# Gate columns in a recurrence tile that is worked first, and 512-column products for the recurrence's output

## What is computed

```python
proj = h @ w_in
(rx, rgate, q, kc, vc, ks, vs, kw, vw, nsa_g, mg_rnn, mg_attn) = jnp.split(proj, splits, axis=-1)
hr = rg_lru(causal_dwconv(rx, rnn_conv_w, rnn_conv_b), rg_w_a, rg_b_a, rg_w_x, rg_b_x, lru_lambda)
y_rnn = (hr * jax.nn.gelu(rgate)) @ w_rnn_out
o = nsa(q, kc, vc, ks, vs, kw, vw, nsa_g, ...)      # g = sigmoid(gates); g0*o_cmp + g1*o_slc + g2*o_win
y_attn = o @ w_attn_out
x = x + (jax.nn.sigmoid(mg_rnn) * y_rnn + jax.nn.sigmoid(mg_attn) * y_attn) @ w_out
```

## Time and profile before

| | us |
|---|---|
| median of 3 runs | 818.85 (818.69 to 819.10) |
| the profiled execution | 818.65 |
| its span, first to last instruction | 816.9 |

### The profile page before, as it was taken

One profiled execution on the slowest core, in us unless ns is written; L12 is line 12 of the kernel. 1 busy time (PEld: TensorE's weight loads), 2 busy tenths in 40 slices (PEclk: granted clock), 3 DMA queues, 4 the chain that ended last, 5 costly groups with the idle time before them and its releaser, 6 DMA issues.

```text
span 816.9 us, 12246 instructions
## 1 busy us (share of the span) xinstructions
PE 806.0 (99%) x4997; PEld 705.7 (86%) x4997; DVE 588.0 (72%) x751; ACT 481.8 (59%) x730; POOL 31.3 (4%) x46
## 2 busy tenths in 40 slices
PE   9999999999999999999999999999999999999996
PEld 8889898889899998988888888888888988888885
DVE  5684597898966775798787868877877655654555
ACT  6463687878757444675666556446654644544551
POOL 1103000000000000000000000020110000000000
PEclk9999999999999999999999999999999999999998
DMA  8436442332434674446555554674443555555431
GB/s 329 155 125 261 164 170 101 120 115 106 154 119 159 228 275 164 142 168 213 200 172 189 206 203 162 234 258 148 155 178 133 207 206 186 179 214 195 162 148 51
DMA packets 22631, 144.00 MB, mean 176 GB/s; under 512 B 2608, under 2 KB 3120, under 8 KB 8240
## 3 DMA queue, kind: packets, MB, share of 16 engines
q1 hardware_dynamic: 20880, 137.92, 47.6%
q10 hardware_dynamic: 1696, 5.31, 1.8%
HBM read 142.17 MB, written 1.05 MB: 175 GB/s over the span
## 4 chain that ended last, share of the span: by engine, by line
PE 92%; ACT 3%; DVE 3%; issue 1%; POOL 0%; DVEq 0%; POOLq 0%; ACTq 0%
PE PS L1689 19%; PE PS L1693 10%; PE PS L1742 10%; PE PS L1743 10%; PE PS L1746 10%; PE PS L1676 7%; PE PS L1677 6%; PE PS L1681 6%; PE PS L1705 2%; PE PS L1836 1%; PE PS L2006 1%; PE PS L1802 1%; PE PS L1813 1%; PE PS L1713 1%; DVE WL L1040 1%
## 5 line engine op out<-in xcount | busy, mean ns | idle before, releaser
L1040 DVE TENSOR_TENSOR WL<-RAW,WH 128x2048 fp32r<-128x2048 f32 (+2 forms) x128 | 285.2, 2229 | 45.5 <-ACT WH L614 45.5
L614 ACT ACTIVATE WH<-RAW 128x2048 fp32r<-128x2048 f32 (+2 forms) x128 | 238.8, 1867 | 67.5 <-PE PS L1746 26.5
L1445 DVE TENSOR_TENSOR HLS<-PS,HLS 128x512 f32<-128x512 f32 x46 | 31.7, 689 | 92.7 <-ACT HLS L945 92.7
L1689 PE MATMUL PS<-CHL,WH 128*128 128x512 f32 x352 | 87.9, 392 | 0.0
L1676 PE MATMUL PS<-BHL,WH 128*126 128x256 f32 (+2 forms) x344 | 85.6, 287 | 0.4 <-ACT TI L785 0.4
L1677 PE MATMUL PS<-BHL,WH 128*126 128x256 f32 (+2 forms) x344 | 83.6, 282 | 0.0
L945 ACT ACTIVATE HLS<-PS 128x512 f32<-128x512 f32 x46 | 27.4, 595 | 90.8 <-PE PS L1693 86.3
L1689 PE MATMUL PS<-BHL,WH 128*128 128x512 f32 x320 | 79.9, 392 | 0.0
L1689 PEld LDWEIGHTS PS<-CHL,WH 128*128 128x128 f32 x352 | 63.9, 189 | 11.8
L1676 PEld LDWEIGHTS PS<-BHL,WH 128*126 128x126 f32 (+2 forms) x344 | 64.3, 187 | 5.2 <-issue 4.3
L1743 PE MATMUL PS<-WH,AL 128*128 128x512 f32 x176 | 68.7, 391 | 0.0
(11 more groups left out here) (312 smaller groups left out, 1374.9 us busy)
## 6 DMA issues: line engine op xcount, KB each, us to landing
RAW<-in_w_stream SPq DMA_DIRECT2D x108, 1024.0 KB, 4.8
RAW<-in_w_stream SPq DMA_DIRECT2D x11, 1008.0 KB, 4.8
RAW<-in_w_stream SPq DMA_DIRECT2D x8, 704.0 KB, 4.3
WF<-in_w_stream SPq DMA_DIRECT2D x2, 1024.0 KB, 5.0
LN<-in_ln ACTq DMA_DIRECT2D x2, 1024.0 KB, 5.3
WF<-in_w_stream SPq DMA_DIRECT2D x4, 294.0 KB, 2.8
X<-in_x SPq DMA_DIRECT2D x2, 512.0 KB, 4.2
RAW<-in_w_stream SPq DMA_DIRECT2D x2, 512.0 KB, 7.2
```

The costliest lines, as they stand in the source:

```text
L614: eng.activation(WH[:, c % NSLOT, 0:CHUNKS[c][2]], raw(c), ACT.Copy).then_inc(w_hi, 1)
L1040: eng.tensor_tensor(WL[:, c % NSLOT, 0:CHUNKS[c][2]], raw(c), f32(WH[:, c % NSLOT, 0:CHUNKS[c][2]]), ALU.subtract).then_inc(w_lo, 1)
L1445: eng.tensor_tensor(HLS[:, n % 4, :, :], PS[:, bank:bank + 2, 0:TOK], HLS[:, n % 4, :, :], ALU.add)\
L1689: eng.matmul(PS[:, bank, :], wh, HL[:, k, :, :].rearrange("p a t -> p (a t)"), start=(k == 0), stop=False)
```

## The change

The gate chunk goes. Its 48 columns are put, 24 each, in rows 96 to 119 of the two halves (rx and rgate) of rnn tile 4, which is moved to the front of the recurrence, behind w1 1. W0 is now that tile, and the order is rnn 4, rnn 0, rnn 1, mg 0, ri 0, rnn 2, rnn 3, mg 1, ri 1; from there on it is as before. ACT applies the Tanhs at the end of window 0, once DVE's conv steps of that tile are done; PE transposes them in window 1, DVE makes `gts` in window 2. GTT is zeroed on DVE. The rows' waits count tiles in the new order (`RNN_NO`, `RNN_THROUGH`). For group 0, A, squares and roots fall in window 5, and the exponentials of the compressed scores in window 4. Key transposes of cmp 1 use banks 2 and 3 as those of cmp 0 do. AH and AL lie side by side in AHL; a ro chunk is 11 products of 512 columns and 11 of 256, and DVE adds both halves in three steps.

The diff, cut to its core (left out: the new waits on `RNN_NO` and `RNN_THROUGH`, sizes, the packing of the weights):

```diff
@@ -39,6 +39,9 @@
 RG_OF = [(g, t) for g, n in enumerate(RG_TILES) for t in range(n)]
+GATE_TILE = RG_AT[RG_TILES.index(3)] + 2
+GATE_ROW = 96
+GATE_COLS = 24
@@ -89,14 +92,14 @@
     out += [("cmp", i, CHUNK, True) for i in range(2)]
-    out += [("gate", 0, KD * 3 * NH, True)]
...
     out += [("w1", i, CHUNK, False) for i in range(2)]
+    out += [("rnn", GATE_TILE, 2 * KD * RP, True)]
...
         out += [("mg", mg + n, CHUNK, True) for n in range(ahead)]
-        out += [("rnn", RG_AT[g] + t, 2 * KD * RP, True) for t in range(RG_TILES[g])]
+        out += [("rnn", i, 2 * KD * RP, True) for i in range(RG_AT[g], RG_AT[g + 1]) if i != GATE_TILE]
@@ -127,7 +130,10 @@
 OFFS = [sum(P * w for _, _, w, _ in CHUNKS[:c]) for c in range(NCH + 1)]
-W0 = AT[("rnn", 0)]
+W0 = AT[("rnn", GATE_TILE)]
+RNN_NO = {i: n for n, i in enumerate(i for kind, i, _, _ in CHUNKS if kind == "rnn")}
+RNN_THROUGH = [max(RNN_NO[i] for i in range(RG_AT[g + 1])) + 1 if g >= RG_TILES.index(3) else
+               max(RNN_NO[i] for i in range(RG_AT[g], RG_AT[g + 1])) + 1 for g in range(NG)]
@@ -198,8 +204,10 @@
+    if step >= 2 and W0 + w - step + 1 == AT["ri", 0]:
+        return 0
     kind, g, _, _ = CHUNKS[max(0, W0 + w - step)]
-    return g if kind == "ri" else None
+    return g if kind == "ri" and (g or step < 2) else None
@@ -259,8 +267,8 @@
         a_at = top[0]
-        AH = put("AH", [P, NA, TOK], F32R)
-        AL = put("AL", [P, NA, TOK], F32R)
+        AHL = put("AHL", [P, NA, 2, TOK], F32R)
+        AH, AL = AHL[:, :, 0, :], AHL[:, :, 1, :]
@@ -664,6 +673,12 @@
                                    accum_out=css[0:NKV * CP, :]).then_inc(kc_sq, 1)
+                    eng.wait_ge(hk_zero, 6)
+                    eng.wait_ge(mb_dve, 1)
+                    for part in range(2):
+                        eng.activation(GTT[32 * part:32 * part + GATE_COLS, :],
+                                       PS[GATE_ROW:GATE_ROW + GATE_COLS, mb_of(MB_NO[W0]), TOK * part:TOK * part + TOK],
+                                       ACT.Tanh, scale=0.5).then_inc(gate_tanh, 1)
@@ -676,6 +691,9 @@
                     eng.activation(SCT[:, :], PS[:, 5, :], ACT.Copy).then_inc(kcz_ready, 1)
+                if w == 4:
+                    eng.wait_ge(sc_sub, 1)
+                    eng.activation(SC[:, :, :, :], SC[:, :, :, :], ACT.Exp).then_inc(sc_exp, 1)
@@ -742,9 +760,6 @@
                         eng.activation(l2[0:RP, :], l1[0:RP, :], ACT.Exp, scale=-1.0).then_inc(lam_exp, 1)
-                if kind == "gate":
-                    eng.wait_ge(chunk_done, c + 1)
-                    eng.activation(GTT[:, :], PS[0:3 * NH, 4, 0:TOK], ACT.Tanh, scale=0.5).then_inc(gate_tanh, 1)
@@ -761,8 +776,10 @@
                         eng.activation(HK[:, 0, :, 0:NC], hidden(0), ACT.Gelu_apprx_tanh).then_inc(hk_ready, 1)
-                if kind == "rnn" and i == 1:
+                if c == W0 + 1:
                     q_copy(1)
+                if c == W0:
+                    eng.wait_ge(q_ss, 2 * NT)
@@ -1007,16 +1024,13 @@
                     split(c + 2)
-                if c == SPLIT_IN_SOFTMAX:
+                if c == SPLIT_AHEAD:
                     split(c + 2)
-                if c - W0 == 4:
-                    eng.wait_ge(sc_sub, 1)
-                    eng.activation(SC[:, :, :, :], SC[:, :, :, :], ACT.Exp).then_inc(sc_exp, 1)
...
                 side(c)
-                if CHUNKS[c][0] == "ri" and c != SPLIT_IN_SOFTMAX:
+                if CHUNKS[c][0] == "ri" and c != SPLIT_AHEAD:
@@ -1150,8 +1164,12 @@
                         last.then_inc(vb_ready, 1)
+                if w == 2:
+                    eng.wait_ge(gate_t_done, 1)
+                    eng.tensor_scalar(gts[:, :].rearrange("p (t a n) -> p t a n", t=NT, a=2),
+                                      PS[:, 4, TOK:2 * TOK - P].rearrange("p (t a n) -> p t a n", t=NT, a=2)[:, :, :, 0:GATE_COLS],
+                                      0.5, 0.5, ALU.mult, ALU.add).then_inc(gate_ready, 1)
                 if w == 3:
-                    split(W0 + w + 2)
@@ -1208,11 +1226,12 @@
                     eng.tensor_tensor(JJ[:, :], ident[:, 0:64], ident[:, 64:P], ALU.add).then_inc(hk_zero, 1)
+                    eng.memset(GTT[:, :], 0.0).then_inc(hk_zero, 1)
...
                     eng.wait_ge(gk_ready, 1)
-                    bank = (2, 6)[i]
+                    bank = 2
@@ -1229,8 +1248,8 @@
                     eng.scalar_tensor_tensor(q, p, -8.0, q, ALU.mult, ALU.add).then_inc(c4_ready, 1)
-                if kind == "gate" or kind == "q" and i == 0:
-                    n = 0 if kind == "gate" else 1
+                if kind == "q" and i < 2:
+                    n = i
@@ -1273,8 +1288,12 @@
                     t = MG[:, i, :]
-                    link(eng.scalar_tensor_tensor(t, t, 1.0, PS[:, bank, 0:256], ALU.add, ALU.mult))
-                    eng.tensor_tensor(t, t, MG[:, 8 + i, :], ALU.add).then_inc(m_ready, 1)
+                    if i >= 1:
+                        eng.wait_ge(m_ready, i)
+                    link(eng.scalar_tensor_tensor(RS2[:, :, :], t.unsqueeze(1).broadcast_to([P, 2, TOK]), 1.0,
+                                                  PS[:, bank, :].rearrange("p (a t) -> p a t", a=2), ALU.add, ALU.mult))
+                    link(eng.tensor_tensor(t, RS2[:, 0, :], MG[:, 8 + i, :], ALU.add))
+                    eng.tensor_tensor(t, t, RS2[:, 1, :], ALU.add).then_inc(m_ready, 1)
@@ -1605,9 +1624,7 @@
                     unit_max(u)
-                if c - W0 == UNIT_WINDOWS[0]:
-                    compressed_weights()
-                if c and CHUNKS[c - 1][0] == "ri" and c - 1 != SPLIT_IN_SOFTMAX:
+                if c and CHUNKS[c - 1][0] == "ri" and c - 1 != SPLIT_AHEAD:
@@ -1615,6 +1632,8 @@
                     rg_log_a(G)
+                if c - W0 == UNIT_WINDOWS[0]:
+                    compressed_weights()
@@ -1631,7 +1650,7 @@
                     rg_second(NG - 1)
-                if CHUNKS[c][:2] not in SUMS_FIRST and kind != "ri":
+                if CHUNKS[c][:2] not in SUMS_FIRST and kind != "ri" or c == SPLIT_AHEAD:
@@ -1858,6 +1877,11 @@
                                   ident[0:NKV * CP, 0:NKV * CP]).then_inc(kct_done, 1)
+                    eng.wait_ge(gate_tanh, 2)
+                    for t in range(NT):
+                        last = eng.transpose(PS[:, 4, TOK + 64 * t:TOK + 64 * t + 64], GTT[:, P * t:P * t + P],
+                                             ident[0:64, 0:64])
+                    last.then_inc(gate_t_done, 1)
@@ -1968,15 +1992,11 @@
                         last = f_tile(PS[:, bank, 256 * j:256 * j + 256], c, 1024 * j, P, BH, BL)
-                if kind == "gate":
-                    eng.wait_ge(const_in, 32)
-                    eng.wait_ge(kn_ready, 2)
-                    eng.wait_ge(k_sq, 2)
-                    last = f_tile(PS[0:3 * NH, 4, 0:TOK], c, 0, 3 * NH, BH, BL)
...
                     if i == 0:
-                        eng.wait_ge(kt_copied, 2)
+                        eng.wait_ge(kn_ready, 2 * NT)
+                        eng.wait_ge(k_sq, 2 * NT)
@@ -1989,6 +2009,8 @@
                 if kind == "rnn":
+                    if c == W0 + 2:
+                        eng.wait_ge(gate_tanh, 2)
@@ -2041,7 +2063,14 @@
                     bank = mb_bank(MB_NO[c])
-                    last = f_tile(PS[:, bank, 0:256], c, 0, P, AH, AL, nk=NR, parts=RP)
+                    s = c % NSLOT
+                    for k in range(NR):
+                        eng.matmul(PS[:, bank, :], WH[0:RP, s, P * k:P * k + P], AHL[0:RP, k, :, :].rearrange("p a t -> p (a t)"),
+                                   start=(k == 0), stop=False)
+                    eng.wait_ge(w_lo, SPLIT_NO[c] + 1)
+                    for k in range(NR):
+                        last = eng.matmul(PS[:, bank, 0:TOK], WL[0:RP, s, P * k:P * k + P], AH[0:RP, k, :], start=False,
+                                          stop=(k == NR - 1))
@@ -2182,8 +2211,6 @@
-                if n == 0:
-                    eng.wait_ge(gate_ready, 1)
@@ -2195,22 +2222,19 @@
                 if kind == "cmp":
+                    eng.wait_ge(const_in, 32)
                     eng.wait_ge(kn_ready, 2 * i + 2)
+                    if i:
+                        eng.wait_ge(kt_copied, 1)
...
                             o = 256 * (g % 2) + P * t
-                            last = eng.transpose(PS[:, (2, 6)[i] + g // 2, o:o + P],
+                            last = eng.transpose(PS[:, 2 + g // 2, o:o + P],
...
                     last.then_inc(kt_done, 1)
-                if kind == "q" and i == 0:
-                    eng.wait_ge(gate_tanh, 1)
-                    for t in range(NT):
-                        last = eng.transpose(PS[:, 4, TOK + 3 * NH * t:TOK + 3 * NH * t + 3 * NH], GTT[:, P * t:P * t + P],
-                                             ident[0:3 * NH, 0:3 * NH])
-                    last.then_inc(gate_t_done, 1)
...
                     q_transposes(0)
```

(28 more changed lines are left out.)

## The result

The kernel after takes 820.46 us (median of 17 runs, 819.2 to 821.31), the kernel before in the same session 818.85 (17 runs, 818.69 to 819.96). The ratio is 1.0016, 95% interval 1.001 to 1.0023: slower by 1.6 us. The interval leaves out 1, so the loss is real, but it is small: 0.16%. The forecast was 817.3 with a range up to 818.9. The kernel after also scatters over 2.1 us, while 15 of the 17 runs of before lie within 0.41 us; the reason for that turns out to be part of the loss. The profiled execution of after took 819.2 us (span 817.5), which is the fastest of its 17, so its trace shows less of the loss than the other runs have.

A forecast was written before the change was run, and what follows sets the result against it. PE was taken as the bound, busy 806.0 of 816.9 us. Terms -3.31 + 0.3 + 2.85 - 0.43 - 0.96 = -1.55 took the profiled 818.65 to 817.10; 0.20 for the median gave 817.3 us, range 815.2 to 818.9.

The forecast's parts named there:

- Part 3: Window 1, the main step: PE waits for ACT's q copy, queued behind the Tanhs and mg 0's split; +2.85 us.
- Part 1: Ahead of W0: gate chunk and its transposes go, so PE reaches W0 3.31 us earlier; q 0's load hidden.
- Part 2: Window 1: the gates' two transposes return on PE, +0.3 us (0 to 0.5).
- Part 4: Ahead of rnn 2: PE's stall for the bank ACT reads goes, -0.43 us (-0.43 to 0).
- Part 5: Recurrence output: a ro chunk goes from 3.96 to 3.84 us, saving 0.96 us for 8; DVE's added work fits.
- Part 6: Windows 3 to 7: reordered work adds nothing, 1.5 us slack ahead of mg 1; unit 3's 0.4 us stall stays.
- B: Rival, window 1: the wait is short or absent; 814.5 us, or 815.9 with half of it; chance 0.14.
- C: Rival, ro chunks: DVE becomes their bound, slower; 822.6 us at 4.5 us a chunk; chance 0.08.
- D: Rival, ro chunks: the output change does nothing, chunks stay at 3.96 us; 818.3 us; chance 0.08.

The follow-up runs named there:

- experiment 8: Kernel after with PE's start-up products changed from 14 of 128 columns to 13 of 128 and 16 of 8, 60 more PE instructions: 818.46 us, ratio 0.9997.
- experiment 3: Kernel after with thirty unused transposes of a constant on PE ahead of its wait in window 1: 818.33 us, ratio 0.9995.
- experiment 5: Kernel before with only the change's ro output part (11 products of 512 columns, 11 of 256, three DVE steps): 817.69 us, ratio 0.9988.
- experiment 1: Kernel after with ACT's copy of the transposed q moved into window 0, ahead of the gates' Tanhs and the split of mg 0: 814.70 us, ratio 0.9951.
- experiment 9: Kernel after with both the copy of q ahead of the Tanhs and 60 more PE instructions at the start: 814.02 us, ratio 0.9943.
- experiment 6: Kernel after with the recurrence's output part undone, 33 products of 256 columns in a ro chunk again: 821.81 us, ratio 1.0038.

## Why the prediction was wrong

The mechanism forecast as the main step is what happened: the change wins at the gate chunk, at rnn 2 and in ro, and pays it back in window 1, behind the copy of q. Two terms were wrong, one in size and one by its absence.

**Part 3, the size.** 2.85 us forecast, 3.84 measured in after, 4.4 and 4.6 in two relatives. The step that failed is that part 3 goes "by the times of before; all of it shifts by the same 3.31", which carries the landing at 82.00 over unchanged; the rivals defend it with "the same load, queue and trigger as before". The load's trigger moved with the work, but the code load that it shares the DMA engines with did not, and the load landed 0.85 us later than the shift said. With the code load out of the way (experiment 8) the wait is 2.97, 0.12 over the forecast.

**The clock, missing.** The prediction reads the granted clock once, finds 1.00, and from then on prices a wait at its own length. It adds a wait of 2.85 us to a kernel whose longest standing of PE in this part was 0.43 us, and doesn't ask what the clock does behind it. So the step that failed is a term put at nothing: the clock behind the wait. It costs some 1.4 us in the profiled execution of after and 2.1 at the median (experiment 3). No row of before could give that price, since the clock never falls there in this stretch; but the range should have had an end for it, and has none. Even with the right wait it would have been needed: experiment 8 has 2.97 us, and seven of its 11 runs show the fall by their times and mean clocks.

The two together: 817.3 + 1.0 + 2.1 = 820.4, measured 820.46. The 2.1 is itself the difference of two medians, 820.46 and 818.33, so what this sum tests is the rest: 817.3 + 1.0 = 818.3 against the 818.33 of experiment 3. And where neither acts, in the four runs of experiment 8 at a mean clock of 0.997, the time is 817.1, against 818.71 for the kernel before beside it: 1.6 us less, where the sum says 1.55.

**Part 1**: W0 3.26 us earlier, forecast 3.31. Right, q 0 starts at 45.52 and its load is hidden. **Part 2**: with the clock at 1.00 the transposes and what stands with them take 89.30 to 90.19, 0.89, in experiment 3, against 0.69 before (88.40 to 89.09): 0.20, forecast 0.3. **Part 4**: no idle time ahead of rnn 2 (108.52, behind unit 0's products at 107.44). Right. **Part 5**: 3.83 us a chunk forecast as 3.84, 0.98 us in all against 0.96 (experiment 5). The Trainium skill ("TensorE: Matmul & The Clock Gate", Back-to-back issue gap), by an estimate from its figure for an isolated product, had 0.2 us; the trace disagrees, and the two rows of the same form were the better guide. DVE takes the third step: ro 6 and 7 do run late with it, and wo 0 absorbs that. The timeline of DVE behind ro 7 in after shows it still in the split while wo 0 runs:

```profile
301.31 2.28 DVE L1054 TENSOR_TENSOR WL<-RAW,WH 128x2048 fp32r<-128x2048 f32 x1
303.51 0.68 DVE L1293 SCALAR_TENSOR_TENSOR RS<-MG,PS 128x512 f32<-128x512 f32 x1
```

**Part 6**: no wait ahead of mg 1, and the 0.4 us behind unit 3's exponentials stays. Right as to its claim. Its sum has a small slip: 20.3 - 1.9 - 0.85 - 3.1 is 14.45, not 14.3, which leaves 1.35 us of slack instead of 1.5; in after DVE's conv of rnn 2 ends at 120.43 and PE begins mg 1 at 121.51, 1.1 us of slack. Between the chunk behind window 1 and 158 us after makes good some 0.9 of the 2.5 us that it has lost by 97.34, of which the stall at rnn 2 is 0.43. The rest comes in small pieces between chunks and was not followed further.

**Rivals.** B (a short wait) did not come by itself; experiment 1, which makes it by hand, gives 814.7 where B said 814.5. C fell: ro chunks are 3.83 apart. D fell in experiment 5. No table load stands between the Gelu of HVX and the gates' Tanh (82.04 to 85.24 on ACT).

## What to carry to other kernels

Where PE is the bound, a wait has two prices: its length, and what the clock does behind it. A wait of 0.4 us had only the first in every run here; from 2 us on the second came in most runs, by their times and mean clocks, and could be as large as the wait. So in an in-order queue the copy that PE wants next belongs ahead of everything that waits for another engine: moving one ACT instruction was worth 5.8 us, more than the 4.7 us that the whole change brings at its best (experiment 9). A landing time may be carried over from one trace to the next only if everything on the same DMA engines moves along with the load; the code loads, which go by PE's instruction count, don't.

## What the hardware showed unexpectedly

Whether the clock falls behind a wait differs from run to run of one kernel. Behind 2.06 us of standing it fell in 7 of 11 runs by their times and mean clocks, behind 2.97 us in 7 of 11, behind 3.84 us in the profiled execution and, by mean clocks of 0.993 to 0.996, in all 17 runs. Behind 0.41 us, and behind 0.88 us that followed work put into the gap, it fell in none. Once fallen, it stayed at 1.2 GHz for about 3 us of full work in after, and until 96 us in the profiled execution of experiment 6, for more than 5 us of work. With thirty transposes of a constant in the gap it did not fall.

With one 16 KB packet of instructions under way, a 1 MB load landed 0.8 to 1.5 us later, and of its sixteen shares only the last was late. It is not so each time: over the whole trace of after the last share came 0.40 us behind the fifteenth at the median of the 32 weight loads that met such a packet, and 0.04 us for the other 104; in the other traces the first median lies between 0.07 and 0.49, the second between 0.02 and 0.05. This made the time of a kernel depend on how many instructions PE had done before, by 0.7 us (experiment 9 against 1) to 2.0 us (experiment 8 against after).
